# Expert 0's rows selected from contiguous columns, the token halves on two array tiles, the sum formed by the turning products

## What is computed

```python
def ec_moe(x, router_w, w_gate, w_up, w_down):
    cap = n_tok * EC_CAPACITY // N_EXPERTS          # 64 of 512 sample tokens, 16 of 128 prompt tokens
    aff = softmax(einsum('btd,de->bte', x, router_w))
    gate, idx = lax.top_k(swapaxes(aff, 1, 2), cap)
    xe = x[bidx, idx]
    hid = silu(einsum('becd,edf->becf', xe, w_gate)) * einsum('becd,edf->becf', xe, w_up)
    ye = einsum('becf,efd->becd', hid, w_down) * gate[..., None]
    return zeros_like(x).at[bidx, idx].add(ye)

xm = rms_norm(x, norm2_w) * (1 + sc2) + sh2
x = x + g2 * ec_moe(xm, ...)
```

## Time and profile before

| | us |
|---|---|
| median of three runs (1416.03 to 1419.14) | 1416.8 |
| the profiled execution's own time | 1415.48 |
| its span, first to last instruction | 1413.6 |
| PE busy in the span | 1324.3 (94%) |
| ACT busy | 529.4 (37%) |
| DVE busy | 698.1 (49%) |
| mean granted PE clock | 0.982 |

### The profile page before, as it was taken

The page is one execution under the profiler, slowest core; times in us unless marked ns, Lnnn a source line. Parts: engine busy times, 40 slices in busy tenths (PEclk is TensorE's granted clock), DMA queues, the critical chain, the costliest instruction groups (busy, mean ns, idle before and its releaser), DMA issues. The chain is left out here.

```text
span 1413.6 us, 27174 instructions
## 1 busy us (share of the span) xinstructions
PE 1324.3 (94%) x11105; PEld 806.2 (57%) x11105; DVE 698.1 (49%) x1636; ACT 529.4 (37%) x1221; POOL 276.8 (20%) x237
## 2 busy tenths in 40 slices
PE   5999998889899999999989999989899999999995
PEld 1756566766686444444438998555588444444443
DVE  1536514677635333344357628866735344333435
ACT  2723113676333322222225468665523322222213
POOL 0001104596002011111100040555301011111101
PEclk7999999999999999999999999999999999999997
DMA  9688860131437999999982022050053999999985
GB/s 364 232 327 333 331 217 25 37 144 46 182 119 258 369 374 374 375 374 376 388 294 77 4 69 60 1 223 1 14 225 112 373 378 376 374 375 379 374 312 179
DMA packets 105799, 333.80 MB, mean 236 GB/s; under 512 B 23182, under 2 KB 29164, under 8 KB 99532
## 3 DMA queue, kind: packets, MB, share of 16 engines
q1 hardware_dynamic: 99276, 310.11, 57.9%
q0 software_dynamic: 5824, 19.86, 6.0%
q10 hardware_dynamic: 576, 2.10, 0.4%
HBM read 308.13 MB, written 23.89 MB: 235 GB/s over the span
## 5 line engine op out<-in xcount | busy, mean ns | idle before, releaser
L1957 PE MATMUL psum<-wraw,proj 128*32 128x512 f32 x3072 | 403.0, 598 | 7.7 <-issue 6.0
L1963 PE MATMUL psum<-wraw,proj 128*16 128x256 f32 x3072 | 235.6, 381 | 0.6 <-ACT proj L2071 0.6
L1963 PEld LDWEIGHTS psum<-wraw,proj 128*16 128x16 f32 x3072 | 90.2, 97 | 232.2 <-issue 227.4
L1957 PEld LDWEIGHTS psum<-wraw,proj 128*32 128x32 f32 x3072 | 96.8, 110 | 79.7 <-issue 15.8
L1925 POOL DMA_INDIRECT x_rows<-modrow,idx x30 | 42.9, 1429 | 452.6 <-DVE modrow L2166 452.6
L2084 ACT ACTIVATE proj<-psum 128x320 f32<-128x320 f32 x32 | 14.0, 437 | 286.5 <-PE psum L2023 286.5
L2128 DVE TENSOR_SCALAR proj<-psum,proj 128x64 f32<-128x64 f32 x232 | 55.6, 312 | 107.0 <-PE psum L1945 107.0
L1336 POOL TENSOR_SCALAR ring<-ring,small 128x640 f32<-128x640 f32 x48 | 90.3, 1886 | 39.8 <-DVE small L1275 39.4
L2161 DVE SCALAR_TENSOR_TENSOR modrow<-psum,proj 64x512 f32<-64x512 f32 x60 | 45.0, 749 | 84.2 <-PE psum L1963 83.8
L2153 DVE TENSOR_TENSOR proj<-proj,psum 64x512 f32<-64x512 f32 x32 | 22.1, 690 | 127.5 <-ACT proj L2091 127.5
L1266 DVE TENSOR_REDUCE small<-psum 128x1 f32<-128x640 f32 (+1 forms) x80 | 57.3, 717 | 52.3 <-PE psum L1241 51.8
(11 more groups left out here) (519 smaller groups left out, 2410.6 us busy)
## 6 DMA issues: line engine op xcount, KB each, us to landing
wraw<-in_exp_w_gate_dram SPq DMA_DIRECT2D x128, 512.0 KB, 16.4
wraw<-in_exp_w_up_dram SPq DMA_DIRECT2D x128, 512.0 KB, 16.8
wraw<-in_exp_w_down_dram SPq DMA_DIRECT2D x128, 512.0 KB, 16.5
ring<-in_ada_w_dram SPq DMA_DIRECT2D x29, 1024.0 KB, 6.9
hold<-in_ada_w_dram SPq DMA_DIRECT2D x14, 1024.0 KB, 6.8
ring<-in_ev_w_in_dram SPq DMA_DIRECT2D x4, 2048.0 KB, 12.3
xr<-x_rows SPq DMA_DIRECT2D x15, 512.0 KB, 7.5
proj<-in_ada_w_dram SPq DMA_DIRECT2D x5, 1024.0 KB, 9.1
```

The source lines that it names most:

```text
L1957: mm = pe.matmul(psum[quad(q, 32), b, :], xs[:, quad(q % 2, 32)], pair[q // 2], start=first, stop=last)
L1963: mm = pe.matmul(psum[quad(q, CAPP), b, 0:QP], xs[:, CAPS:CAP], pair[q // 2][:, q % 2 * QP:(q % 2 + 1) * QP], start=first, stop=last)
```

## The change

Five things change, in both layers.

1. **The products that select.** All four `pick` matrices must be there before the first product. For each half `h` of the channels (512 contiguous columns) tiles 0 and 1 are summed on the left array tile and tiles 2 and 3 on the right one. Half 0 goes to bank 0, half 1 to bank 1. PSUM partitions 0 to 63 then hold the sum over half of the tokens and 64 to 127 the sum over the others.
2. **The copy to SBUF.** ACT copies two banks (128 x 512 each) where it copied one, the first as soon as half 0 is through.
3. **The turn.** Four transposes become eight products (`tensor_rows`): the stationary operand is `rows[:, k::KD]`, 128 columns in steps of 32 bytes, the moving one is `both_halves`, two 64 x 64 identities one above the other. So each product turns one channel group and adds the two partial sums. A small DVE instruction makes `both_halves` early in `out_l`.
4. **Order and places.** The results lie in banks 5 and 6; the order of the `k` steps, the banks of the prompt part and the semaphore counts follow. SP's load 8 now waits for both halves.
5. **Keepers.** The counts of `keep_busy` stay; the second one writes to bank 4 instead of bank 5.

```diff
+            both_halves = small[:, 64:64 + CAPS]
...
-                sp.wait_ge(selected, 1)
+                sp.wait_ge(selected, 2)
...
-                for t in range(ST):
-                    pe.wait_ge(s["pick"], t + 1)
-                    for c in range(2):
-                        mm = pe.matmul(psum[64 * c:64 * c + CAPS, 1, :], pick[:, t, :], columns(t, 4 * c, 4 * c + 4), start=(t == 0), stop=(t == ST - 1))
-                    if t == ST - 2:
-                        turn_affinities(pe, 1)
-                mm.then_inc(selected, 1)
-                keep_busy(pe, 5, 5)
+                pe.wait_ge(s["pick"], ST)
+                for h in range(2):
+                    for j in range(2):
+                        for c in range(2):
+                            t = 2 * c + j
+                            mm = pe.matmul(psum[64 * c:64 * c + CAPS, h, :], pick[:, t, :], xr[:, t, h * 512:(h + 1) * 512], start=(j == 0), stop=(j == 1))
+                        if h == 1 and j == 0:
+                            turn_affinities(pe, 1)
+                    mm.then_inc(selected, 1)
+                keep_busy(pe, 5, 4)
+
+            def tensor_rows(pe, rows):
+
+                for k in range(KD):
+                    at = k // 2 * CAPS
+                    mm = pe.matmul(bank(5 + k % 2)[:, at:at + CAPS], rows[:, k::KD], both_halves, start=True, stop=True)
+                return mm
...
-                    mm = pe.matmul(psum[32 * q:32 * q + 2 * CAPP, 3, 0:256], pick_p, columns(PT, 2 * q, 2 * q + 2), start=True, stop=True)
+                    mm = pe.matmul(psum[32 * q:32 * q + 2 * CAPP, 1, 0:256], pick_p, columns(PT, 2 * q, 2 * q + 2), start=True, stop=True)
...
+                            own(dve.tensor_tensor(both_halves, ident[:, 0:CAPS], ident[:, CAPS:2 * CAPS], ALU.add))
...
-                    pe.wait_ge(s["selc"], 1)
-                    for k in range(4):
-                        mm = pe.transpose(bank(k // 2)[:, k % 2 * P:(k % 2 + 1) * P], picked_s[:, k, :], ident[:, :])
-                    mm.then_inc(s["xT"], 2)
+                    pe.wait_ge(s["selc"], 2)
+                    routed["tensor_rows"](pe, picked_s).then_inc(s["xT"], 2)
...
-                    for n, k in enumerate((0, 4, 1, 5, 2, 6, 3, 7)):
+                    for n, k in enumerate((0, 2, 4, 6, 1, 3, 5, 7)):
...
-                act.wait_ge(s["sel"], 1)
-                act.activation(picked_s, bank(1).rearrange("p (k d) -> p k d", k=4), ACT.Copy).then_inc(s["selc"], 1)
+                for h in range(2):
+                    act.wait_ge(s["sel"], h + 1)
+                    act.activation(picked_s[:, h * 512:(h + 1) * 512], bank(h), ACT.Copy).then_inc(s["selc"], 1)
```

More of the change, by code:

```diff
@@ L1531, in sync_after @@
                 load_weights(sp, l, 9, ready)
-            spread = bank(6)[:, 256:256 + CAPS + 2 * CAPP]
+            spread = bank(6)[:, 256:256 + CAPS]
             def columns(t, a, b):
                 return xr[:, t, :].rearrange("p (d k) -> p k d", k=KD)[:, a:b, :]
+            spread_p = bank(7)[:, 64:64 + 2 * CAPP]
             def tensor_choice(pe, selected):
@@ L1563, in tensor_chosen @@
                 for e in range(2):
-                    at = CAPS + CAPP * e
-                    pe.matmul(spread[:, at:at + CAPP], ident[0:NE, e:e + 1].to_broadcast([NE, P]), idxf[0:NE, CAPS:CAP], start=True, stop=True)
+                    pe.matmul(spread_p[:, e * CAPP:(e + 1) * CAPP], ident[0:NE, e:e + 1].to_broadcast([NE, P]), idxf[0:NE, CAPS:CAP], start=True, stop=True)
                 pe.transpose(bank(7)[0:CAP, 0:NE], idxf[0:NE, :], ident[0:NE, 0:NE])
@@ L1591, in vector_chosen @@
                 dve.wait_ge(s["it"], 4)
-                dve.tensor_scalar(pick_p, spread[:, CAPS:CAPS + 2 * CAPP], token_of[:, PT:TILES], rstd[:, PT:TILES], ALU.is_equal, ALU.mult).then_inc(s["pick"], 1)
+                dve.tensor_scalar(pick_p, spread_p, token_of[:, PT:TILES], rstd[:, PT:TILES], ALU.is_equal, ALU.mult).then_inc(s["pick"], 1)
                 dve.tensor_copy(idx[CAPS:CAP, :], bank(7)[CAPS:CAP, 0:NE]).then_inc(s["chosen"], 1)
@@ L1808, in _ @@
                     for t in range(ST):
-                        dve.tensor_scalar(pick[:, t, :], spread[:, 0:CAPS], token_of[:, t:t + 1], rstd[:, t:t + 1], ALU.is_equal, ALU.mult).then_inc(s["pick"], 1)
+                        dve.tensor_scalar(pick[:, t, :], spread, token_of[:, t:t + 1], rstd[:, t:t + 1], ALU.is_equal, ALU.mult).then_inc(s["pick"], 1)
                     then["vector"](dve, own)
@@ L2183, in vector @@
                 dve.wait_ge(s["xT"], 2)
-                for k in (2, 6, 3):
+                for k in (1, 3, 5):
                     modulate_picked(k)
```

27 lines of the change are left out of this document (14 added, 13 removed).

## The result

| | before | changed |
|---|---|---|
| median of 17 runs each, us | 1416.8 (1414.1 to 1423.4) | 1423.8 (1413.8 to 1426.8) |
| ratio to before | | 1.0039, 95% interval 1.0022 to 1.0055 |
| profiled execution, us | 1415.48 | 1413.76 |
| its span, us | 1413.6 | 1411.9 |
| its mean granted PE clock | 0.982 | 0.985 |

The interval lies beyond the 0.2% of the prediction, so the change costs time, about 7 us by the medians. The reader must be warned about the profile: the one execution that was recorded is the fastest of the 17. The other 16 lie between 1417.0 and 1426.8, and their time goes with the mean granted clock: 1417.0 at 0.982, 1419.6 at 0.977, 1421.4 at 0.976, 1426.4 at 0.969. A page that shows 0.985 doesn't show what the median paid. What it shows well is the place of the change when the clock is full.

A forecast was written before the change was run, and what follows sets the result against it. It took the weights to bound the expert stages: 3.16 us saved less 1.44 for the turn starts expert 0 1.7 us earlier per layer, worth nothing in layer 0 and 0.6 in layer 1, so 1416.2 us; range 1413.4 to 1418.4.

The forecast's parts named there:

- What bounds the kernel: Expert stages: PE and DMA are both full; weights end layer 0's stage and lead by only 0.6 us in layer 1.
- Rival A: Expert stages: all of PE's 1.7 us earlier start reaches the end in both layers, 1413.4 us; chance 0.15.
- Start and products: Selecting products: start 0.76 us later, passes at 0.43 instead of 0.92 us save 3.92, so the keepers come 3.16 earlier.
- The copy: ACT's two copies after selection: the first beside the second half's products, the second under the keepers; costs nothing.
- The turn: Transposes replaced by eight products ahead of expert 0: twelve more weight loads at 0.12 us each cost 1.44 us.
- rival B: Turning products: strided loads cost 0.23 us each, 16 take 3.7 us and eat the gain; 1416.8 us; chance 0.14.
- rival C: Layer 0's expert stage: one long weight wait lowers the clock, 3.0 us lost; 1419.2, up to 1422 us; chance 0.09.
- Behind that wait stand only the products themselves: Start of the selecting products: one wait for all four picks delays only these products, by 0.76 us.
- Slower executions may well hold longer waits for weights: Whole execution: those slower than the profiled 1415.48 us may wait longer for weights, making the gain smaller, not larger.

The follow-up runs named there:

- e3_ordered_copy: The changed kernel, but ACT's copy writes the channels already in groups, so the turning products load contiguous columns; 1416.0 us, 0.9992 of before.
- e4_select_alone: The kernel before with only the selecting products reading contiguous columns, turned by four transposes as before, channels in another order; 1417.5 us, 0.9999 of before.
- f3_ordered_filled: The changed kernel with ACT's copy writing grouped channels and three more keepers ahead of the wait for the picks; 1416.9 us, 0.9997 of before.
- the wide turn: The changed kernel with 256 instead of 64 moving columns in each turning product; 1419.3 us, 1.0015 of before, and 1418.1 us, 1.0008 when repeated.
- f1_filled_wait: The changed kernel with three more keepers ahead of the wait for the four picks; 1417.3 us, 1.0011 of before.

## Why the prediction was wrong

- **What bounds the kernel: right.** The weights set the end of an expert stage, and earlier arrival turns into waits for them. `e3_ordered_copy` and `e4_select_alone` show it with gains of 1.8 and 3.9 us a layer that leave the time within 0.1% of before. Where PE did come about 1.8 us earlier, the waits were those of the prediction (2.2 us in layer 0, 1.1 in layer 1): 2.2 in layer 0 of `e3_ordered_copy`, 2.1 and 1.3 in `f3_ordered_filled`. Rival A is refuted: with the gain of `e4_select_alone` it would give 1409, and its own ratio of 0.9976 lies just outside the interval of `e3_ordered_copy` (from 0.9977).
- **Start and products: right.** First pick to first product went from 0.46 to 1.15 us, so 0.69 later (said: 0.76); from there to the keepers 3.94 us instead of 7.81, so 3.87 saved (said: 3.92). The keepers come 3.18 us earlier against the picks (said: 3.16).
- **The copy: right.** 446.70 + 0.60 = 447.30 lies before the first turning load at 447.69.
- **The turn: the term that was mis-sized.** "Twelve more loads cost 12 x 0.12 = 1.44 us" was 3.3: from the first turning load to expert 0's first product it is 452.30 - 447.69 = 4.61 us, and was 453.86 - 452.56 = 1.30. I took the price of a strided load from line 1945, and those are transposes, which take one pass (they also have 64 partitions and not 128, and no run tells which of the two matters). A load for a float32 product in 32-byte steps costs 0.24 us, close to rival B's 0.23. With it, 3.18 - 3.31 = -0.13 us: no gain at all, which is rival B as to the mechanism. The Trainium skill ("SBUF — State Buffer", section "Door 1: The DMA port swizzle"), by whose rule such loads should pay as strided moving columns do, was right for them: the trace agrees with it for products (0.24 instead of 0.12) and not for the transposes of line 1945. I gave rival B 0.14 with rows 6 against it; it should have been the forecast, since nearest in kind to these loads was not a transpose's load but the strided float32 product next door.
- **The clock: the mechanism that was missing.** Rival B's time was 1416.8, and the median is 7 us above it. I looked for a fall behind a long wait for weights in layer 0 (rival C, up to 1422) and let the 3.7 us of rival B's turn stand as busy time. The time goes with the mean clock (0.973 over 43 executions, 0.979 over 124 of before), and the ordered copy, the wide turn or three more keepers, each a local edit, bring 5 to 11 us of it back on their chips. The one profile of the changed kernel above 1420 us shows the clock fall behind exactly that stretch and at the selecting products, for 7.2 us, and in layer 1's attention for 4.4 more. The prediction's step "Behind that wait stand only the products themselves" left out that these products may run at 1.2 GHz. Rival C had the right sign and the wrong place; the median is not within the range given (1413.4 to 1418.4).
- **"Slower executions may well hold longer waits for weights"** was the place to ask what makes an execution slow. The three runs of before that were known spread over 3.1 us. Over its later 124 executions the time follows the mean clock (1415.8 us at 0.981, 1424.4 at 0.970, by a straight line), and the changed kernel is more often at the low end. I read the scatter as noise around a fixed sum.

What stays open. The share of each place in the 7 us isn't settled: either remedy gives back most of it, both together no more, and one profiled execution each is too few to count falls. The attention of layer 1 is a third place, and no kernel was made to test it. Why the shorter wait doesn't help where three keepers do isn't settled either; one reading is that work ahead of the products matters more than the length of the gap, but no kernel tried that alone. Nor did one change the router's products ahead of the keepers, which the expectation of `f1_filled_wait` names as the rival; that 7 of the falls at the picks began in the keepers speaks for looking there. And at an equal clock the changed kernel is perhaps a microsecond or two above before (by a straight line through each kernel's executions, 1417.7 against 1415.8 at about 0.981), which these runs don't explain.

## What to carry to other kernels

Price a strided stationary operand by a load of the same kind of instruction: of a float32 product with one of a product, never with a transpose's. Where PE's part ahead of a saturated stage changes, count lateness in full and earliness as nothing until the weights' lead is known. Look at the granted clock behind a new stretch of back-to-back loads too, although it shows as 100% busy: here it fell behind 5 of 16 such stretches. When executions spread by more than the effect, compare their mean granted clocks first, and don't explain a median by one profile whose clock is above theirs, nor by a sum of two places before the rest of the span has been compared.

## What the runs showed that was not expected

- Weight loads of 128 columns for float32 products take 0.24 us in 32-byte steps (3.88 us for 16) and 0.12 us contiguous (1.86 for 16), while those of transposes, with 64 partitions instead of 128, took 0.12 in the same steps.
- PE at 100% busy does not keep its clock: 3.40 us with 15 products of 64 columns and 3.26 us of loads were followed by a window at 0.50. With 256 columns behind each load, 0.2 us longer in all, no such fall was recorded, and 24 executions had a median of 1418.3 instead of 1424.9.
- All five profiled executions above 1420 us have a fall in layer 1's attention (16.0 to 19.0 us where the others take 14.3), among them one whose turn is before's.
- An execution's time is set largely by how often the clock falls: the changed kernel's straight line goes from 1417.7 us at 0.981 to 1426.5 at 0.970, before's from 1415.8 to 1424.4. The first, profiled execution of a kernel was the fastest of its 17.
